# Two gate units of each long convolution in three-product form, with the split of the normalised activations woven around the convolution loop

## The chip, the core and the metric

The kernel runs on one core of a Trainium2 chip. The metric is device time in microseconds (us) from the start to the end of one execution; lower is better. The engines named below are TensorE (PE, matmuls), VectorE (DVE), ScalarE (ACT), GpSimd (POOL) and SyncE (SP, which here only issues the weight transfers). Each has its own queue, executed in the order written, and they meet through semaphores.

## What is computed

A stack of five blocks over 256 positions of width 1024, all in float32: a long-convolution mixer, a forgetting-attention mixer, a short-convolution mixer, a second long-convolution mixer, and a last block with three kinds of attention and a feed-forward part. The change touches the two long-convolution mixers alone. One of them, cut to what matters:

```python
def conformer_conv_mixer(h, w_in, conv_w, conv_b, ln_g, ln_b, w_out):   # h = rms_norm(x), 256 x 1024
    proj = h @ w_in                                   # 1024 x 6144
    val, glu_gate, z = jnp.split(proj, 3, axis=-1)    # 2048 channels each
    u = val * jax.nn.sigmoid(glu_gate)
    u = causal_depthwise_conv(u, conv_w) + conv_b     # 31 taps
    u = jax.nn.silu(layer_norm(u, ln_g, ln_b))        # over the 2048 channels
    return (u * jax.nn.silu(z)) @ w_out               # 2048 x 1024
```

## The kernel before

Activations lie transposed: channels on the partitions, the 256 positions along the free axis. So the 2048 channels of a mixer are 16 tiles of 128 x 256 (`c` = 0 to 15), and the 1024 channels of `x` are eight. Weights come in units of 1 MB (1024 x 256) through `ring`, three slots; SP issues the transfer of a unit when the unit three places before it is used up. A unit holds two halves of 128 output channels.

A product with a unit has two forms. In the **plain** form TensorE multiplies the float32 unit in `ring` by the float32 activations `sqb` (L783): 16 matmuls, each of which the profile records as two. In the **split** form both sides are first written as a high part, rounded to the type fp32r, and a low part, the difference. ACT casts a half of the unit to `whi` (L371, 128x1024), DVE or POOL subtracts to get `wlo` (L380, 128x1024), and TensorE makes three products for each of the 8 tiles of `x`: whi by xh, whi by xl, wlo by xh. That is 48 matmuls for a unit. `whi` and `wlo` have four places, so a half is cast ahead by at most four. The activations are split in four steps of two tiles: a cast to `xh` on ACT and a subtraction to `xl` on DVE (`norm_low`, 128x512, both inputs in SBUF, in blocks other than this one).

A long-convolution mixer (`plan_conf`, `conf_pe`, `conf_act`, `conf_dve`, `conf_pool`; `j` = 0 for the first, 1 for the second) has three parts.

1. **The loop** over `c`. TensorE makes value and gate of tile `c` (units `vg`, plain); ACT takes the sigmoid, DVE multiplies to `up`. The 31 taps are shared: DVE adds up 20 of them in PSUM (L1191), ACT scales the other 11 (L1043) into four buffers `tmp`, and POOL adds those (L1101, and L1104 as the last, which counts `pool_sum`). DVE joins the two sums (`join`); the last tile, 15, is joined at L1147 and L1149. ACT squares each finished tile (L1022), and TensorE adds tiles and squares over the channels two tiles at a time (`pair_sums(q)`, L1256); `pair_sums(7)` needs tile 15. Beside that, TensorE makes the eight units `z` (gate of the output): two within the loop, six behind it.
2. **Statistics**, beside units `z[4]` and `z[5]`. ACT copies the sums (L1057), TensorE turns them (`stats_turned`, L1261 and L1262), DVE reduces them and makes the variance (L1207 to L1210), ACT takes the root (L1059, behind an `ACT_TABLE_LOAD`), DVE the reciprocal, and TensorE spreads mean and factor to all partitions (`spread(0)`, `spread(1)`, L1266). The places of these matmuls among those of `z[5]` are written as `at_k={(half, k): ...}`.
3. **The y loop** over the 16 tiles, in pairs `q` on DVE: `centre` (L1225) and multiply by the factor (L1237), then ACT's silu (L1072), then POOL's product with silu(z) into the three slots `yr` (L1110), then ACT's cast to `y_hi` (`y_high`, L958), then DVE's subtraction to `y_lo` (`y_low`, L962). POOL may write a slot only when the `y_low` three tiles before is done. Into the same loops are written the splits of the first two units of `w_out` (`OUT_BESIDE`: unit 0 at c = 8, unit 1 at c = 13), two casts on ACT and two subtractions on DVE each. The splits of the other units of `w_out` come behind the loops. TensorE meanwhile makes `z[5]`, `z[6]`, `z[7]` and then the eight units of `w_out` (L865 to L867, split), 5.8 us each.

## Time and profile before

| | |
|---|---|
| median of 3 runs | 1489.11 us (1487.85 to 1490.62) |
| the profiled execution | 1488.68 us |
| its span, first to last instruction | 1486.8 us |
| TensorE | 1463.6 us busy, 98% |
| VectorE | 1063.7 us, 72% |
| ScalarE | 843.3 us, 57% |
| GpSimd | 470.1 us, 32% |
| mean granted TensorE clock | 0.997 of full speed |
| first long convolution | about 10 to 238 us of the span |
| second long convolution | about 742 to 962 us |

The busy shares are averages over all blocks. What a change is worth has to be read at its own place, from the order of time of each engine there, from the waits, and from the chain of work that ended last: that chain is followed back from the last instruction, at each step to what released it.

### The profile page before, as it was taken

Reading aid. Unit: us, or ns where it says so; the run is one execution under the profiler, and the core shown is the slowest. Engines: PE = TensorE matmul, PEld = TensorE weight load, DVE = VectorE, ACT = ScalarE, POOL = GpSimd, SP = SyncE. Lnnn points to the kernel's source line nnn. Section 1 sums busy time; section 2 is a strip of 40 time slices with the busy share of each in tenths; the row PEclk is TensorE's granted clock in tenths of the full one; section 3 lists DMA queues with packets and bytes.
Section 4 is the critical chain, followed back from the end, with each engine's and each line's share of the span. In section 5 each row is a group of like instructions: output and inputs, shape, how many; then the busy total and the mean of one; then the engine's idle time right before and its main releaser. Section 6 shows DMA issues by size and latency. Waiting matters only on the chain.

```text
span 1486.8 us, 24998 instructions
## 1 busy us (share of the span) xinstructions
PE 1463.6 (98%) x9231; PEld 1299.2 (87%) x9231; DVE 1063.7 (72%) x2225; ACT 843.3 (57%) x1612; POOL 470.1 (32%) x447
## 2 busy tenths in 40 slices
PE   8999999999999999999999999999999999999999
PEld 6888899998889988889988888999887778988887
DVE  5899767455787698887599997565257677786632
ACT  4567766445666555555456777454336756556542
POOL 2778613433333200000057883054421002000033
PEclk9999999999999999999999999998999999999999
DMA  7554355766644567876454445563852224576653
GB/s 212 150 165 149 126 188 173 232 168 151 129 142 151 158 186 208 220 196 200 143 142 142 142 142 170 185 165 114 213 158 86 86 86 141 148 205 187 173 196 112
DMA packets 308110, 239.40 MB, mean 161 GB/s; under 512 B 18018, under 2 KB 286708, under 8 KB 307989
## 3 DMA queue, kind: packets, MB, share of 16 engines
q1 hardware_dynamic: 295816, 228.70, 52.7%
q10 hardware_dynamic: 12172, 9.10, 2.7%
q8 instruction: 74, 1.21, 0.4%
q14 instruction: 48, 0.39, 0.1%
HBM read 236.02 MB, written 1.75 MB: 160 GB/s over the span
## 4 chain that ended last, share of the span: by engine, by line
PE 65%; DVE 24%; issue 5%; ACT 4%; POOL 2%; DMA 1%; DVEq 0%; POOLq 0%; SPq 0%; ACTq 0%
PE bank L805 12%; DVE bank L1191 11%; PE bank L807 6%; PE bank L865 3%; PE bank L867 3%; PE bank L866 3%; DVE wlo L380 3%; PE bank L783 3%; PE bank L1719 3%; PE bank L1721 3%; PE bank L1720 3%; PE bank L2079 2%; PE bank L1346 2%; PE bank L828 2%; PE bank L787 1%
## 5 line engine op out<-in xcount | busy, mean ns | idle before, releaser
L380 POOL TENSOR_TENSOR wlo<-ring,whi 128x1024 fp32r<-128x1024 f32 x89 | 222.4, 2506 | 861.7 <-ACT whi L371 861.7
L371 ACT CAST whi<-ring 128x1024 fp32r<-128x1024 f32 x330 | 338.4, 1046 | 193.9 <-PE bank L1721 49.5
L380 DVE TENSOR_TENSOR wlo<-ring,whi 128x1024 fp32r<-128x1024 f32 (+1 forms) x241 | 296.2, 1249 | 147.0 <-ACT whi L371 146.3
L783 PE MATMUL bank<-sqb,ring 128*128 128x256 f32 x1504 | 331.8, 380 | 1.0 <-DVE sqb L662 0.8
L783 PEld LDWEIGHTS bank<-sqb,ring 128*128 128x128 f32 x1504 | 283.7, 190 | 47.7 <-issue 6.4
L805 PE MATMUL bank<-xhl,whi 128*128 128x512 f32 x768 | 269.1, 395 | 1.3 <-DVE xhl L708 1.3
L1191 DVE SCALAR_TENSOR_TENSOR bank<-scratch,convw,bank 128x256 f32<-128x256 f32 x600 | 240.6, 484 | 0.0
L1101 POOL TENSOR_TENSOR scratch<-scratch 128x256 f32<-128x256 f32 x288 | 199.7, 732 | 98.4 <-ACT scratch L1043 74.8
L807 PE MATMUL bank<-xhl,wlo 128*128 128x256 f32 x768 | 215.2, 280 | 0.0
L805 PEld LDWEIGHTS bank<-xhl,whi 128*128 128x128 f32 x768 | 143.9, 187 | 35.0 <-issue 2.0
L1043 ACT ACTIVATE scratch<-scratch,convw 128x256 f32<-128x256 f32 x320 | 146.2, 499 | 47.8 <-POOL scratch L1101 47.0
L865 PE MATMUL bank<-y_hi,whi 128*128 128x256 f32 x512 | 146.1, 285 | 1.8 <-DVE wlo L380 1.8
L807 PEld LDWEIGHTS bank<-xhl,wlo 128*128 128x128 f32 x768 | 145.1, 189 | 0.0
L866 PE MATMUL bank<-y_lo,whi 128*128 128x256 f32 x512 | 144.8, 283 | 0.0
L867 PE MATMUL bank<-y_hi,wlo 128*128 128x256 f32 x512 | 144.8, 283 | 0.0
L1719 PE MATMUL bank<-xhl,whi 128*128 128x256 f32 x384 | 110.2, 287 | 0.8 <-DVE qk L1679 0.8
L1720 PE MATMUL bank<-xhl,whi 128*128 128x256 f32 x384 | 108.6, 283 | 0.0
L1721 PE MATMUL bank<-xhl,wlo 128*128 128x256 f32 x384 | 108.5, 283 | 0.0
L865 PEld LDWEIGHTS bank<-y_hi,whi 128*128 128x128 f32 x512 | 98.2, 192 | 2.7 <-ACT whi L371 2.1
L866 PEld LDWEIGHTS bank<-y_lo,whi 128*128 128x128 f32 x512 | 98.2, 192 | 0.1
L867 PEld LDWEIGHTS bank<-y_hi,wlo 128*128 128x128 f32 x512 | 98.2, 192 | 0.0
L1394 ACT ACTIVATE scratch<-scratch,small 128x128 f32<-128x128 f32 (+1 forms) x120 | 50.9, 425 | 46.8 <-DVE small L1384 46.8
(322 smaller groups left out, 2747.8 us busy)
## 6 DMA issues: line engine op xcount, KB each, us to landing
ring<-in_a_w_in_dram SPq DMA_DIRECT2D x64, 512.0 KB, 5.2
ring<-in_b_w_in_dram SPq DMA_DIRECT2D x32, 1024.0 KB, 6.0
ring<-in_c_w_in_dram SPq DMA_DIRECT2D x64, 512.0 KB, 5.3
ring<-in_w_in_dram SPq DMA_DIRECT2D x26, 1024.0 KB, 5.2
ring<-in_w_ffn_in_dram SPq DMA_DIRECT2D x44, 512.0 KB, 5.0
ring<-in_a_w_in_dram SPq DMA_DIRECT2D x16, 1024.0 KB, 5.1
ring<-in_a_w_out_dram SPq DMA_DIRECT2D x16, 1024.0 KB, 5.4
ring<-in_w_ffn_out_dram SPq DMA_DIRECT2D x10, 1024.0 KB, 5.0
```

Source lines behind the costliest of these rows:

```text
L371: nc.scalar.copy(piece(whi, h)[:, :, 0:n], src).then_inc(hi_done, 1)
L380: engine.tensor_tensor(piece(wlo, h)[:, :, 0:n], src, piece(whi, h)[:, :, 0:n].bitcast(F32), ALU.subtract).then_inc(done, 1)
L783: mm = nc.tensor.matmul(o, halves[h][1][:, k, :], sqb[:, k, :], start=(k == 0), stop=(k == KD - 1))
L805: nc.tensor.matmul(o[:, :], wh[:, k, :], xhl[:, k, :, :].rearrange("p s t -> p (s t)"), start=(k == 0), stop=False, skip_group_check=True)
L807: mm = nc.tensor.matmul(o[:, 0:S], wl[:, k, :], xh[:, k, :], start=False, stop=(k == KD - 1), skip_group_check=True)
L865: nc.tensor.matmul(o, wh[:, k, :], hi[:, kk, :], start=first, stop=False, skip_group_check=True)
L866: nc.tensor.matmul(o, wh[:, k, :], lo[:, kk, :], start=False, stop=False, skip_group_check=True)
L867: mm = nc.tensor.matmul(o, wl[:, k, :], hi[:, kk, :], start=False, stop=end, skip_group_check=True)
L1101: nc.gpsimd.tensor_tensor(to, a, tmp[:, (first + i) % 4, :], ALU.add)\
L1191: ins = nc.vector.scalar_tensor_tensor(to[:, a, :], src, w, to[:, a, :], ALU.mult, ALU.add)
L1719: nc.tensor.matmul(o, wh, xh[:, k, :], start=first, stop=False, skip_group_check=True)
L1720: nc.tensor.matmul(o, wh, xl[:, k, :], start=False, stop=False, skip_group_check=True)
```

## The change

- Units `z[6]` and `z[7]` of both mixers are made in split form (`Z_SPLIT`). All four low parts of the unit halves are DVE's.
- The activations are therefore split in this block too: the four casts to `xh` stand on ACT in the loop, behind the taps of tiles 8, 9, 11 and 12 (`X_HIGHS`); three of the four subtractions to `xl` stand on DVE ahead of the join of tile 15, the fourth behind it.
- ACT casts the first half of `z[6]` between the squares of tiles 14 and 15, the second half behind the load of the root's table, both halves of `z[7]` behind the root. DVE subtracts the first half of `z[6]` ahead of the statistics, and the other three in the y loop, at q = 1, 2 and 3 (`Z_LOWS`).
- ACT copies the sums ahead of the load of the root's table, not behind it, and `stats_turned`, `spread(0)` and `spread(1)` stand two plain matmuls (four recorded ones) earlier in `z[5]`.
- The calls `act_ahead` and `dve_ahead` of the loop stay only for tile 0 of the second mixer; at the others they issued nothing.
- `RESPLIT`, the list by which the splits of the activations are counted, has all six blocks now; the one wait written with a fixed number follows it.

```diff
+        Z_SPLIT = (6, 7)
...
-                n["z"].append((free, unit_in(w, [(2 * E + i * 2 * P, 2 * P)], plain=True)))
+                n["z"].append((free, unit_in(w, [(2 * E + i * 2 * P, 2 * P)], ALL if i in Z_SPLIT else False, plain=(i not in Z_SPLIT))))
...
-        RESPLIT = (1, 2, 4, 5)
+        RESPLIT = (0, 1, 2, 3, 4, 5)
...
+        X_HIGHS = (8, 9, 11, 12)
...
+                if c in X_HIGHS:
+                    g = X_HIGHS.index(c)
+                    act.wait_ge(xr_done, KD * n["ph"] + 2 * g + 2)
+                    if j == 1:
+                        group_done(act, n["vg"][0][1])
+                    nc.scalar.copy(xh[:, 2 * g:2 * g + 2, :], sqb[:, 2 * g:2 * g + 2, :]).then_inc(xh_done, 1)
...
-            for c in range(KE - 2, KE):
-                square(c)
+            square(KE - 2)
+            hi_to(act, first_half[n["z"][6][1]])
+            square(KE - 1)
             conf_z(act, n, 4)
-            nc.scalar.activation(l_warm, eps, ACT.Sqrt)
             act.wait_ge(sqm_done, (j + 1) * (KE // 2))
             nc.scalar.copy(x_sums, bank[7][:, 0:S]).then_inc(mean_done, 1)
+            nc.scalar.activation(l_warm, eps, ACT.Sqrt)
+            hi_to(act, last(n["z"][6][1]))
             act.wait_ge(var_done, j + 1)
             nc.scalar.activation(l_var, l_var, ACT.Sqrt, bias=eps).then_inc(lstd_done, 1)
+            hi_to(act, last(n["z"][7][1]))
...
+            for g in range(3):
+                norm_low(dve, n["ph"], g)
             join(len(TILE_GROUPS) - 1)
+            norm_low(dve, n["ph"], 3)
+            lo_dve_to(dve, first_half[n["z"][6][1]])
             dve.wait_ge(stat_tr, j + 1)
...
+            Z_LOWS = {1: last(n["z"][6][1]), 2: first_half[n["z"][7][1]], 3: last(n["z"][7][1])}
...
             for q in range(KE // 2 + 2):
+                if q in Z_LOWS:
+                    lo_dve_to(dve, Z_LOWS[q])
...
-            proj_T(pe, *n["z"][5], at_k={(0, 2): lambda: pair_sums(7), (0, 7): stats_turned, (1, 3): lambda: spread(0), (1, 6): lambda: spread(1)})
-            proj_T(pe, *n["z"][6])
+            proj_T(pe, *n["z"][5], at_k={(0, 2): lambda: pair_sums(7), (0, 5): stats_turned, (1, 1): lambda: spread(0), (1, 4): lambda: spread(1)})
+            proj_T(pe, *n["z"][6], True, n["ph"])
             proj_T(pe, *n["z"][7])
```

How the queues stand at the three places that matter. First DVE in the first mixer, from the last taps to the fourth pair of the y loop. Before (L1147 and L1149 are the join of tile 15, L1207 the first step of the statistics, L1225 `centre`, L1237 the multiplication, L962 `y_low`):

```order
L1191 SCALAR_TENSOR_TENSOR bank<-scratch,convw,bank 128x256 x12
L1147 TENSOR_TENSOR wide<-bank,scratch 128x256
L1149 TENSOR_TENSOR wide<-bank,wide 128x256
L1207 TENSOR_REDUCE small<-bank 128x4
...
L1225 TENSOR_TENSOR wide<-wide,bank 128x512 x3
L1237 TENSOR_TENSOR wide<-wide,bank 128x512
L1225 TENSOR_TENSOR wide<-wide,bank 128x512
L1237 TENSOR_TENSOR wide<-wide,bank 128x512
L962 TENSOR_TENSOR y_lo<-yr,y_hi 128x256
```

The same place on DVE with the change (L710 is `norm_low`, L1160 and L1162 the join, L1224 the statistics, L1242 `centre`, L1257 the multiplication, L964 `y_low`):

```order
L1204 SCALAR_TENSOR_TENSOR bank<-scratch,convw,bank 128x256 x12
L710 TENSOR_TENSOR xhl<-sqb,xhl 128x2x256 x3
L1160 TENSOR_TENSOR wide<-bank,scratch 128x256
L1162 TENSOR_TENSOR wide<-bank,wide 128x256
L710 TENSOR_TENSOR xhl<-sqb,xhl 128x2x256
L380 TENSOR_TENSOR wlo<-ring,whi 128x1024
L1224 TENSOR_REDUCE small<-bank 128x4
...
L1257 TENSOR_TENSOR wide<-wide,bank 128x512
L380 TENSOR_TENSOR wlo<-ring,whi 128x1024
L1242 TENSOR_TENSOR wide<-wide,bank 128x512
L1257 TENSOR_TENSOR wide<-wide,bank 128x512
L964 TENSOR_TENSOR y_lo<-yr,y_hi 128x256
L380 TENSOR_TENSOR wlo<-ring,whi 128x1024
```

Three subtractions have come ahead of the join, two instructions between it and the statistics, and a subtraction of a unit half ahead of the second, third and fourth pair.

Second, ACT at the statistics of the first mixer. Before (L990 is silu of z, L1022 a square, L1055 the load of the root's table and a dummy root, L1057 the copy of the sums, L1059 the root, L1072 the silu of the y loop):

```order
L1022 ACTIVATE scratch<-wide 128x256 x2
L990 ACTIVATE wide<-bank 128x512
L1055 ACT_TABLE_LOAD
L1055 ACTIVATE small<-small 128x1
L1057 COPY rr<-bank 128x256
L1059 ACTIVATE small<-small 128x2
L1072 ACT_TABLE_LOAD
```

With the change, on ACT (L1025 is the square, L993 silu of z, L1066 the copy, L1067 the table and the dummy, L1070 the root, L1084 the silu of the y loop):

```order
L1025 ACTIVATE scratch<-wide 128x256
L371 CAST whi<-ring 128x1024
L1025 ACTIVATE scratch<-wide 128x256
L993 ACTIVATE wide<-bank 128x512
L1066 COPY rr<-bank 128x256
L1067 ACT_TABLE_LOAD
L1067 ACTIVATE small<-small 128x1
L371 CAST whi<-ring 128x1024
L1070 ACTIVATE small<-small 128x2
L371 CAST whi<-ring 128x1024 x2
L1084 ACT_TABLE_LOAD
```

The copy has moved ahead of the table load, and four casts of unit halves stand around it and the root.

Third, TensorE in `z[5]`. Before (L1256 is the end of `pair_sums(7)`, L1261 and L1262 `stats_turned`, L1266 the two spreads, L783 plain matmuls, L865 the first of `w_out`):

```order
L1256 MATMUL bank<-scratch,cst 32x256 x2
L783 MATMUL bank<-sqb,ring 128x256 x5
L1261 MATMUL bank<-cst,rr 128x128
L1262 MATMUL bank<-cst,rr 128x128
L783 MATMUL bank<-sqb,ring 128x256 x4
L1266 MATMUL bank<-scratch,cst 128x256
L783 MATMUL bank<-sqb,ring 128x256 x3
L1266 MATMUL bank<-scratch,cst 128x256
L783 MATMUL bank<-sqb,ring 128x256 x33
L865 MATMUL bank<-y_hi,whi 128x256
```

And with the change, on TensorE (L785 is the plain matmul, L1281, L1282 and L1286 are the statistics, L789 to L791 the three products of the split form):

```order
L1276 MATMUL bank<-scratch,cst 32x256 x2
L785 MATMUL bank<-sqb,ring 128x256 x3
L1281 MATMUL bank<-cst,rr 128x128
L1282 MATMUL bank<-cst,rr 128x128
L785 MATMUL bank<-sqb,ring 128x256 x4
L1286 MATMUL bank<-scratch,cst 128x256
L785 MATMUL bank<-sqb,ring 128x256 x3
L1286 MATMUL bank<-scratch,cst 128x256
L785 MATMUL bank<-sqb,ring 128x256 x3
L789 MATMUL bank<-xhl,whi 128x256
L790 MATMUL bank<-xhl,whi 128x256
L791 MATMUL bank<-xhl,wlo 128x256
```

Three plain matmuls now stand between the pair sums and `stats_turned` where five stood, and 96 split matmuls stand where 32 plain ones did.

## Rows read from the trace of the kernel before

**Rows 1.** The page: the chain that ended last, share by engine.
```profile
PE 65%; DVE 24%; issue 5%; ACT 4%; POOL 2%; DMA 1%; DVEq 0%; POOLq 0%; SPq 0%; ACTq 0%
```

**Rows 2.** TensorE in order: start, us, engine, line, operation, count, idle time before and releaser.
```profile
168.63 0.41 PE L1256 MATMUL bank<-wide,cst 128*32 128x256 f32 x2 [0.61 <-ACT scratch L1022]
...
175.57 14.41 PE L783 MATMUL bank<-sqb,ring 128*128 128x256 f32 x66
...
193.04 0.28 PE L865 MATMUL bank<-y_hi,whi 128*128 128x256 f32 x1
193.16 0.28 PE L866 MATMUL bank<-y_lo,whi 128*128 128x256 f32 x1
...
202.62 0.36 PE L865 MATMUL bank<-y_hi,whi 128*128 128x256 f32 x1 [0.89 <-DVE wlo L380]
```

**Rows 3.** The chain that ended last, 182 to 203 us: start, us, what.
```profile
182.48 0.61 DVE wide L1237
183.11 0.61 ACT wide L1072
183.81 0.77 POOL yr L1110
...
185.00 0.95 ACT whi L371
...
200.18 1.05 ACT whi L371
201.25 1.24 DVE wlo L380
```

**Rows 4.** DVE in order of time, 160 to 187 us.
```profile
160.24 4.79 DVE L1191 SCALAR_TENSOR_TENSOR bank<-scratch,convw,bank 128x256 f32<-128x256 f32 x12
167.16 0.42 DVE L1147 TENSOR_TENSOR wide<-bank,scratch 128x256 f32<-128x256 f32 x1 [2.13 <-POOL scratch L1104]
...
171.88 0.17 DVE L1207 TENSOR_REDUCE small<-bank 128x4 f32<-128x8 f32 x1 [3.85 <-PE bank L1262]
...
178.97 0.49 DVE L962 TENSOR_TENSOR y_lo<-yr,y_hi 128x256 fp32r<-128x256 f32 x1 [0.72 <-ACT y_hi L958]
...
181.20 0.68 DVE L962 TENSOR_TENSOR y_lo<-yr,y_hi 128x256 fp32r<-128x256 f32 x1 [0.19 <-ACT y_hi L958]
...
185.98 2.36 DVE L380 TENSOR_TENSOR wlo<-ring,whi 128x1024 fp32r<-128x1024 f32 x2 [0.81 <-ACT whi L371]
```

**Rows 5.** ACT in order of time, at the statistics.
```profile
170.40 0.35 ACT L1057 COPY rr<-bank 128x256 f32<-128x256 f32 x1
172.68 0.30 ACT L1059 ACTIVATE small<-small 128x2 f32<-128x2 f32 x1 [1.93 <-DVE small L1210]
```

**Rows 6.** POOL in order of time: the adds of tile 15, and one product.
```profile
160.10 6.22 POOL L1101 TENSOR_TENSOR scratch<-scratch 128x256 f32<-128x256 f32 x9 [0.23 <-DVE wide L1145]
166.40 0.73 POOL L1104 TENSOR_TENSOR scratch<-scratch 128x256 f32<-128x256 f32 x1
...
195.86 1.47 POOL L1110 TENSOR_TENSOR yr<-wide 128x256 f32<-128x256 f32 x1 [2.04 <-ACT wide L1072]
```

**Rows 7.** DVE twice, POOL once: the same four subtractions in two other blocks.
```profile
531.00 2.49 DVE L708 TENSOR_TENSOR xhl<-sqb,xhl 128x512 fp32r<-128x512 f32 x4
...
989.14 6.45 DVE L708 TENSOR_TENSOR xhl<-sqb,xhl 128x512 fp32r<-128x512 f32 x4 [2.84 <-ACT xhl L704]
988.66 2.37 POOL L380 TENSOR_TENSOR wlo<-ring,whi 128x1024 fp32r<-128x1024 f32 x1 [1.65 <-ACT whi L371]
```

**Rows 8.** ACT, then DVE, in order of time, where tile 12 enters the loop.
```profile
116.44 1.28 ACT L990 ACT_TABLE_LOAD   x1
...
120.06 0.42 DVE L1131 TENSOR_TENSOR scratch<-bank,scratch 128x256 f32<-128x256 f32 x1 [0.57 <-ACT scratch L1011]
```

**Rows 9.** TensorE in the second long convolution, in order of time.
```profile
893.26 0.41 PE L1256 MATMUL bank<-wide,cst 128*32 128x256 f32 x2 [0.63 <-ACT scratch L1022]
...
900.20 14.41 PE L783 MATMUL bank<-sqb,ring 128*128 128x256 f32 x66
```

7 lines of the change are left out of this document (4 added, 3 removed).

## The prediction

> **What bounds the kernel now.** The page's busy shares would name TensorE, and the shares of the chain name it too, but they give VectorE a quarter of the chain [rows 1]. So the place of the change is read by itself, in four steps.
>
> First, TensorE in order of time. From the end of the loop to the output product it waits twice: 0.61 us for the square of tile 15 and 0.89 us for a low part of w_out's third unit [rows 2]. In between it is busy with the plain matmuls of z[5] to z[7]. That is the picture of an engine with next to no slack, and it invites the sum "cheaper z units, earlier end".
>
> Second, what released the wait of 0.89 us. The chain through this stretch does not run over TensorE at all: it goes from a multiplication on DVE to the silu on ACT, the product on POOL, the cast on ACT, a cast and a subtraction of a unit half, and so on, until ACT casts the third unit of w_out at 200.18 us and DVE subtracts it at 201.25 us [rows 3]. That cast stands behind the whole y loop in ACT's queue. So the third unit of w_out starts at the end of the y loop plus 2.4 us, whatever TensorE has done by then. The y loop sets the end; TensorE merely arrives 0.89 us early.
>
> Third, what sets the start of the y loop: the join of tile 15 at 167.16 us, for which DVE waited 2.13 us [rows 4] because POOL's adds of that tile ended at 167.13 us [rows 6]; then square, pair sums and statistics.
>
> Fourth, the second mixer. Its waits and its z stretch are the same (0.63 us, and 66 records in 14.41 us) [rows 9], so each term below counts twice.
>
> **TensorE's own gain.** z[6] and z[7] hold 64 of the 66 recorded plain matmuls: 64 x 14.41/66 = 14.0 us [rows 2]. The 96 split ones come at the spacing of the output product, 193.16 - 193.04 = 0.12 us, so 11.5 us. TensorE has 2.5 us less to do in each mixer, 5.0 us in all. This is worth something only if the y loop ends earlier too.
>
> **The statistics.** Copy, turn and spreads stand four recorded matmuls earlier: 4 x 0.218 = 0.87 us. The copy was done at 170.40 + 0.35 = 170.75 us and the root waited 1.93 us for its input [rows 5], so here it was TensorE's queue that held the statistics back, and moving the places gives -0.87 us at the start of the y loop. Putting the copy ahead of the table load only makes that possible; alone it gives nothing. The cast of the second half of z[6] stands ahead of the root. By the row it ends some 1.05 us behind the dummy root, before or about when the variance is ready, so I take 0 for it.
>
> **The join of tile 15.** Three subtractions of 128x512 now stand ahead of the join. At 2.49/4 = 0.62 us each [rows 7] they need 1.9 us and would fit in the idle 2.13 us [rows 4]. But the same four instructions took 6.45 us, 1.61 us each, while POOL ran a subtraction of its own of 2.37 us [rows 7], and a product on POOL, 0.73 us when alone, took 1.47 us when DVE was in a subtraction [rows 6]. The taps of the loop, which read PSUM and run beside POOL all the time, do not show this. So where both engines work from two inputs in SBUF, one waits for the other. Ahead of the join this hits the worst spot: POOL is in its last two adds and the sum, the work that DVE's join waits for. Taken in turn, three subtractions at 0.6 us and three of POOL's at 6.22/9 = 0.69 us, less the small overlaps at the ends, last about 3.5 us from 165.0 us: the join comes at 168.4 us instead of 167.16 us, **+1.2 us**. Bounds: 0, if they interleave freely, and 3 x 1.61 - 2.13 = +2.7 us, if each is drawn out as in the slow row. I take 1.2, since POOL's pieces here are short, unlike those of the slow row.
>
> The Trainium skill states the mechanism outright (SBUF — State Buffer, Who interferes with whom): a VectorE instruction with two SBUF inputs contends with a GpSimd instruction that reads SBUF, the port pair is locked for a whole instruction, and the other engine blocks. By it the term is +1.2 us as reckoned; without it the term would be 0, and the sum 2.4 us lower over the two mixers. It speaks against this placement, and the three rows agree with it.
>
> The fourth subtraction and the first unit half stand behind the join: 0.6 + 1.2 us, inside the 3.85 us for which DVE waited for the turned sums [rows 4]: 0. If that cover went, they would cost up to 1.8 us.
>
> **The casts to xh in the loop.** Four of about 0.6 us on ACT. Three fall where ACT waits for POOL or TensorE anyway. The one behind tile 9 stands ahead of the first taps of tile 10 and of the table load at 116.44 us, behind which DVE waits 0.57 us for a sigmoid [rows 8]. DVE has no slack there, and what it loses it keeps up to the join. ACT has about 0.3 us of short waits ahead of that load, so I take **+0.2 us**, bounds 0 and 0.6.
>
> **The y loop.** Three subtractions of unit halves stand on DVE at q = 1, 2, 3, 1.14 us each (2.36 us for two with the tail of the last) [rows 4]: +3.4 us ahead of the multiplication at 182.48 us, which is on the chain [rows 3]. DVE was idle 0.72 and 0.19 us there, waiting for ACT [rows 4]; its results would now be ready when it comes, so 0.9 us is absorbed. The low part at 181.20 us took 0.68 us, beside a product on POOL, against 0.49 at 178.97 us [rows 4]; it no longer meets that product: another 0.2 us. Net **+2.3 us**. From that multiplication on the chain goes through ACT, POOL, ACT again and DVE as before [rows 3], and nothing in it gets shorter. Bounds: +1.7, if the 0.81 us that DVE waits at 185.98 us [rows 4] is absorbed as well, and +3.4, if nothing is.
>
> ACT's casts of z[7] follow the root and are over, with a table load of 1.28 us as in [rows 8], by about 176.6 us, before the first silu at 177.1: 0. TensorE needs the low parts of z[6] and z[7] later than DVE makes them: 0. The new ring order only frees slots earlier: 0.
>
> **The sum.** For one mixer: -0.87 + 1.2 + 0.2 + 2.3 = +2.8 us at the end of the y loop, so at the third unit of w_out. Behind that TensorE runs without a wait to the end of the stage and passes the delay on. TensorE's own 2.5 us become waiting: at the pair sums (0.61 us grows to 2.0), at the second unit and at the third. Twice +2.8 = +5.6 us. On the profiled execution's 1488.68 us that is **1494.3 us**. The median of the runs shown is 0.43 us above that execution, which the range takes in.
>
> **The rivals.**
>
> *The contention is mild (22%).* The subtractions ahead of the join fit in the idle 2.13 us. For it: the plain length, 1.9 us. Against: the 6.45 and the 1.47 us. One mixer: -0.87 + 0.2 + 2.3 = +1.6, in all +3.2: 1491.9 us. With the y loop at its lower bound and no cost for the casts it is (1.7 - 0.87) x 2 = +1.7: 1490.4 us.
>
> *The contention is heavy (16%).* The join is 2.7 us late: +4.3 for one mixer, +8.6 in all: 1497.3 us.
>
> *TensorE is the bound after all (14%): faster.* Mechanism: the three subtractions in the y loop vanish into waits of DVE, and the y loop ends 2.5 us earlier, so that TensorE's shorter z units count in full: -5.0 us, 1483.7 us. For it: TensorE waits only 1.5 us in this stretch. Against: it needs the loop to lose 2.5 us, and the only thing that makes it shorter is the 0.87 us. It decides at 3.4 us of idle time of DVE ahead of 182.48 us; the rows show 0.9.
>
> *The change doesn't do what it says.* If the turned sums still waited for something else, such as the copy behind the late pair sums, the -0.87 would be 0 and the sum 1.7 us higher, 1496.0 us. It lies within the range.
>
> **How the numbers follow.** My forecast has 48%, mild contention 22%, heavy 16%, TensorE as the bound 14%. The range leaves out the last and takes in the others with their bounds: from 1490.4 less the scatter of the runs, 1489.0, to 1498.0. A measurement can tell 0.2%, 3.0 us, from no change, so faster is below 1486.1 us and slower above 1492.1. Slower: 47 of the 48, all of the heavy case, and 9 of the 22: 72%. Faster: 13%. Within: 15%.
>
> **What would show it.** In the changed kernel's trace, in each mixer: the wait of DVE at the join gone or shorter and the join itself some 1.4 us later; the subtractions to xl longer than 0.68 us and one of POOL's last adds longer than 0.73 us; TensorE waiting 2 us at the last pair sums; the turned sums at about 172, not 171.5 us; the split z units at 11.5 us; the wait of 0.89 us at the third unit of w_out grown to about 4 us, part of it moved to the second unit, still released by DVE's low part; and that unit starting near 205.4 us. I am wrong if that unit starts before 202.6 us, or if the wait there is gone.

## The result: 0.5% slower, and the profile after

| | before | changed kernel |
|---|---|---|
| median | 1488.57 us (6 runs, 1487.74 to 1490.62) | 1495.57 us (6 runs, 1492.78 to 1498.46) |
| profiled execution | 1488.68 us | 1495.07 us |
| its span | 1486.8 us | 1493.3 us |
| TensorE busy | 1463.6 us | 1461.8 us |
| VectorE busy | 1063.7 us | 1077.0 us |

The ratio is 1.0049, 95% interval 1.0035 to 1.0062: slower by 7.0 us (5.2 to 9.2), where 5.6 us was predicted. TensorE has less to do and the kernel takes longer.

**The join.** First DVE in the changed kernel, first mixer, in order of time (start, us, engine, line, operation, count, idle time before and its releaser), then POOL. L710 are the subtractions to xl, L1160 is the join, L1224 the first step of the statistics, L1257 at 184.77 the multiplication that stood at 182.48 us on the chain [rows 3].

```profile
160.16 4.79 DVE L1204 SCALAR_TENSOR_TENSOR bank<-scratch,convw,bank 128x256 f32<-128x256 f32 x12
164.86 3.52 DVE L710 TENSOR_TENSOR xhl<-sqb,xhl 128x512 fp32r<-128x512 f32 x3
168.30 0.41 DVE L1160 TENSOR_TENSOR wide<-bank,scratch 128x256 f32<-128x256 f32 x1
...
172.16 0.17 DVE L1224 TENSOR_REDUCE small<-bank 128x4 f32<-128x8 f32 x1 [1.25 <-PE bank L1282]
...
177.25 1.22 DVE L380 TENSOR_TENSOR wlo<-ring,whi 128x1024 fp32r<-128x1024 f32 x1
...
179.97 1.21 DVE L380 TENSOR_TENSOR wlo<-ring,whi 128x1024 fp32r<-128x1024 f32 x1
...
183.03 1.21 DVE L380 TENSOR_TENSOR wlo<-ring,whi 128x1024 fp32r<-128x1024 f32 x1
184.17 0.67 DVE L1242 TENSOR_TENSOR wide<-wide,bank 128x512 f32<-128x512 f32 x1
184.77 0.67 DVE L1257 TENSOR_TENSOR wide<-wide,bank 128x512 f32<-128x512 f32 x1
```

```profile
160.00 6.70 POOL L1113 TENSOR_TENSOR scratch<-scratch 128x256 f32<-128x256 f32 x9 [0.21 <-DVE wide L1158]
166.78 1.05 POOL L1116 TENSOR_TENSOR scratch<-scratch 128x256 f32<-128x256 f32 x1
```

DVE no longer waits at the join, as it did for 2.13 us [rows 4]: the three subtractions, 1.9 us of work, took 3.5 us beside POOL, whose last sum took 1.05 us, not 0.73, and whose nine adds took 6.70 us, not 6.22 [rows 6]. Counted from the start of the taps the join comes at 168.30 - 160.16 = 8.14 us, before at 167.16 - 160.24 = 6.92 us [rows 4]: +1.22 us.

**TensorE** in the first mixer. L1276 is `pair_sums(7)`, L789 the first split matmul of z[6], L867 the first product of a matmul group of w_out.

```profile
169.77 0.41 PE L1276 MATMUL bank<-wide,cst 128*32 128x256 f32 x2 [1.84 <-ACT scratch L1025]
...
176.95 0.47 PE L789 MATMUL bank<-xhl,whi 128*128 128x256 f32 x1
...
189.64 0.36 PE L867 MATMUL bank<-y_hi,whi 128*128 128x256 f32 x1 [0.83 <-ACT whi L371]
...
192.97 0.39 PE L867 MATMUL bank<-y_hi,whi 128*128 128x256 f32 x1 [0.59 <-DVE y_lo L964]
...
198.06 0.36 PE L867 MATMUL bank<-y_hi,whi 128*128 128x256 f32 x1 [1.60 <-DVE wlo L380]
...
204.96 0.36 PE L867 MATMUL bank<-y_hi,whi 128*128 128x256 f32 x1 [0.92 <-DVE wlo L380]
```

Two waits of together 1.50 us [rows 2] have become five of together 5.78 us, 4.28 us more: 2.42 us of that is the delay itself, and the rest, 1.9 us, is what is seen of the 2.5 us that TensorE has less to do. The row at 204.96 us is the third unit of w_out, at 202.62 us before [rows 2].

**The second mixer.** The same rows of TensorE, and the busy time of the engines in stretches of 5 us (PEclk is the granted clock).

```profile
899.16 0.41 PE L1276 MATMUL bank<-wide,cst 128*32 128x256 f32 x2 [1.82 <-ACT scratch L1025]
...
899.73 2.49 PE L785 MATMUL bank<-sqb,ring 128*128 128x256 f32 x6
```

```profile
core 0: us, PE busy (x) PEld busy (x) DVE busy (x) ACT busy (x) POOL busy (x), PEclk, DMA share, GB/s
895.00:900.00 5.00, 3.18 (x20) 2.17 (x19) 4.97 (x7) 1.93 (x4) 2.15 (x2) 1.00 0.57 182
900.00:905.00 5.00, 5.00 (x18) 4.03 (x18) 1.97 (x10) 4.17 (x7) 0.00 (x0) 0.66 0.09 28
905.00:910.00 5.00, 5.00 (x32) 4.61 (x30) 4.17 (x6) 3.03 (x4) 0.89 (x1) 1.00 0.10 21
```

Behind TensorE's wait of 1.82 us the granted clock falls: 0.66 in 900 to 905 us, a mix of the two levels, 2.4 and 1.2 GHz. The six recorded matmuls behind the pair sums took 2.49 us, where the same six in the first mixer, at full clock, took 1.56 us (from 170.34 us), and the turned sums, for which the statistics wait, stand right behind them.

**The account.** Since each part begins where the last ends, three distances say where the time went: start of the taps to join, join to first step of the statistics, and from there to the third unit of w_out, behind which TensorE passes any delay on.

| us, first mixer | before | after | difference | predicted |
|---|---|---|---|---|
| taps to join | 6.92 | 8.14 | +1.22 | +1.2 |
| join to statistics (168.30 to 172.16) | 4.72 | 3.86 | -0.86 | -0.87 |
| statistics to third unit | 30.74 | 32.80 | +2.06 | +2.3 |
| casts ahead of the taps | | | 0 | +0.2 |
| sum | | | +2.4 | +2.8 |

The second mixer adds +2.4 us and 1.65 us for the lower clock (join to third unit 38.32 us there, 36.66 in the first). Both: 6.5 us. The two profiled executions differ by 6.4 us, but the rest of their span is not equal either: the short-convolution block, which the change leaves alone, took 3.0 us less in the one execution of before, and other stretches 3.0 us more, 2.3 of it behind the second mixer, where both have some lower clock between 1000 and 1050 us. The kernel before, run again, had the same 221.0 us as the changed kernel from the table load at 523 us to the one at 744 us, where the first trace had 218.0. Over all fourteen traces of this case that block took 218.0 us in four and 221.0 us in ten, with nothing between. So that belongs to the execution, not to the kernel, and I compare distances within a mixer from here on.

### The profile page after: what moved, and what is told of

Its sections match the earlier page's. It is cut to its first block, busy times and chain, and to the rows that moved or that the text cites. A ratio compares the mean times of both kernels' runs of the same rounds, so it can differ in the third digit from the quotient of the medians.

```text
span 1493.3 us, 25180 instructions
## 1 busy us (share of the span) xinstructions
PE 1461.8 (98%) x9295; PEld 1297.6 (87%) x9295; DVE 1077.0 (72%) x2241; ACT 853.4 (57%) x1628; POOL 475.6 (32%) x447
## 3 DMA queue, kind: packets, MB, share of 16 engines
q8 instruction: 74, 1.21, 0.3%
## 4 chain that ended last, share of the span: by engine, by line
PE 68%; DVE 23%; ACT 4%; issue 2%; POOL 1%; DMA 1%; ACTq 1%; DVEq 0%; POOLq 0%; SPq 0%
PE bank L807 12%; DVE bank L1204 10%; PE bank L809 6%; PE bank L785 4%; PE bank L867 3%; PE bank L869 3%; PE bank L868 3%; DVE wlo L380 3%; PE bank L1739 3%; PE bank L1741 3%; PE bank L1740 3%; PE bank L1366 2%; PE bank L2099 2%; PE bank L830 2%; PE bank L789 1%
## 5 line engine op out<-in xcount | busy, mean ns | idle before, releaser
L371 ACT CAST whi<-ring 128x1024 fp32r<-128x1024 f32 x338 | 346.8, 1046 | 193.4 <-PE bank L1741 49.5
L380 DVE TENSOR_TENSOR wlo<-ring,whi 128x1024 fp32r<-128x1024 f32 (+1 forms) x249 | 305.7, 1247 | 146.7 <-ACT whi L371 145.9
L785 PE MATMUL bank<-sqb,ring 128*128 128x256 f32 x1376 | 305.7, 382 | 1.0 <-DVE sqb L664 0.8
L785 PEld LDWEIGHTS bank<-sqb,ring 128*128 128x128 f32 x1376 | 260.4, 191 | 44.6 <-issue 6.4
L807 PEld LDWEIGHTS bank<-xhl,whi 128*128 128x128 f32 x768 | 144.2, 188 | 37.4 <-issue 2.1
L867 PE MATMUL bank<-y_hi,whi 128*128 128x256 f32 x512 | 146.1, 285 | 7.9 <-DVE wlo L380 5.0
L867 PEld LDWEIGHTS bank<-y_hi,whi 128*128 128x128 f32 x512 | 98.2, 192 | 9.4 <-ACT whi L371 7.7
L1739 PEld LDWEIGHTS bank<-xhl,whi 128*128 128x128 f32 x384 | 73.5, 191 | 3.8 <-ACT whi L371 2.5
```

The lines of the kernel that those rows point to most:

```text
L371: nc.scalar.copy(piece(whi, h)[:, :, 0:n], src).then_inc(hi_done, 1)
L380: engine.tensor_tensor(piece(wlo, h)[:, :, 0:n], src, piece(whi, h)[:, :, 0:n].bitcast(F32), ALU.subtract).then_inc(done, 1)
L785: mm = nc.tensor.matmul(o, halves[h][1][:, k, :], sqb[:, k, :], start=(k == 0), stop=(k == KD - 1))
L807: nc.tensor.matmul(o[:, :], wh[:, k, :], xhl[:, k, :, :].rearrange("p s t -> p (s t)"), start=(k == 0), stop=False, skip_group_check=True)
L867: nc.tensor.matmul(o, wh[:, k, :], hi[:, kk, :], start=first, stop=False, skip_group_check=True)
L1739: nc.tensor.matmul(o, wh, xh[:, k, :], start=first, stop=False, skip_group_check=True)
```

## The experiments

The chief measure is **join to third unit**, in us, first and second mixer, beside the ratio to the kernel before, run beside it, with its 95% interval, and the wait of TensorE at `pair_sums(7)` (one number where both mixers have the same). Theory: the loss is DVE and POOL blocking each other ahead of the join (+1.2 us a mixer) plus three low parts in the y loop (+2.1), less the earlier statistics (-0.86); TensorE's shorter units are worth nothing there. Chief rivals: the contention is no part of it, or TensorE's time does count.

| run | join to third unit | wait at pair sums | median us | ratio |
|---|---|---|---|---|
| before again | 35.45 / 35.45 | 0.6 | 1488.16 (one) | |
| change again | 38.30 / 36.67 | 2.4 | 1496.78 | 1.0050 (1.0032 to 1.0068) |
| one SBUF input | 36.67 / 36.66 | 0.65 | 1491.22 | 1.0015 (1.0004 to 1.0027) |
| statistics alone | 34.60 / 34.60 | 0.6 | 1487.10 | 0.9989 (0.9978 to 0.9999) |
| z[6] alone | 34.89 / 34.91 | 1.8, 2.4 | 1490.90 | 1.0019 (1.0005 to 1.0032) |
| two lows on POOL | 39.27 / 39.46 | 1.8, 2.4 | 1500.08 | 1.0075 (1.0056 to 1.0095) |
| split of x alone | 35.46 / 37.15 | 2.4 | 1494.32 | 1.0033 (1.0019 to 1.0047) |
| nothing added on DVE's path | 35.93 / 35.94 | 0.6 | 1489.63 | 1.0000 (0.9988 to 1.0012) |
| five ahead of the join | 35.46 / 35.46 | 2.0 | 1493.79 | 1.0034 (1.0020 to 1.0048) |
| ten ahead of the join | 38.32 / 37.50 | 5.6 | 1500.33 (one) | |
| low parts later | 34.63 / 34.64 | 0.6 | 1485.87 | 0.9989 (0.9977 to 1.0001) |
| statistics earlier still | 34.24 / 34.25 | 0.6 | 1485.29 | 0.9986 (0.9974 to 0.9998) |

### The two kernels again

> The kernel before, unchanged, for a second trace of it. Only 2 x 2.3 us of the 6.5 us by which the changed kernel's span is longer lie at the two third units of w_out (204.96 against 202.62 us in the first mixer). The rest lies elsewhere: +3.0 us in the short-convolution block, whose code is the same, 0.21 us for each of its 14 tiles; +1.7 us in a stretch of the second mixer with a granted clock of 0.91; and -1.3 us where only the trace of before had such a stretch. Theory A, these belong to the single execution: this second trace of the same kernel shows 0.21 us for a tile, or the place of the slow clock stretches, differently from the first. Theory B, they belong to the kernel: this trace shows 11.09 us for a tile of the short block (as before) and the changed kernel's next one 11.30.

> The changed kernel, unchanged, for a second trace of it and three more rounds of times. Theory A (see the run of the kernel before): third unit of w_out at 205.0 us again, since that is set by the order of the queues, but the pace of the short block and the slow clock stretches come out otherwise than in its first trace. Theory B: the short block at 11.30 us for a tile again. Time against before: 1.003 to 1.006 by either; the two queue terms alone give 4.7 us, 1.0031.

The kernel before gave the same distances, the changed one a second pattern. Its DVE, then its POOL, then TensorE, first mixer:

```profile
165.46 1.89 DVE L710 TENSOR_TENSOR xhl<-sqb,xhl 128x512 fp32r<-128x512 f32 x3
169.45 0.42 DVE L1160 TENSOR_TENSOR wide<-bank,scratch 128x256 f32<-128x256 f32 x1 [2.10 <-POOL scratch L1116]
```

```profile
160.61 8.01 POOL L1113 TENSOR_TENSOR scratch<-scratch 128x256 f32<-128x256 f32 x9 [0.22 <-DVE wide L1158]
168.69 0.72 POOL L1116 TENSOR_TENSOR scratch<-scratch 128x256 f32<-128x256 f32 x1
```

```profile
170.93 0.60 PE L1276 MATMUL bank<-wide,cst 128*32 128x256 f32 x2 [2.40 <-ACT scratch L1025]
```

Here DVE's three subtractions ran at full pace, 1.89 us, and POOL was the one held up: nine adds in 8.01 us, not 6.22 [rows 6]. DVE's wait at the join is back, 2.10 us, and looks as if nothing had happened; but the join comes 3.91 us behind the end of the taps, 3.35 us in the first trace of the change, 2.13 us before. So the same code costs 1.2 or 1.8 us here, and who is blocked changes from execution to execution. The third unit, expected at 205.0 us again, came at 207.75 us: the later join is one part of that, and a stretch of lower clock behind the wait of 2.40 us another, 1.6 us (38.30 us against the second mixer's 36.67).

### Is it the two SBUF inputs?

The subtractions to xl take their second input from PSUM, so the low parts of x are not computed: same count, shape and place.

```diff
+            def one_input(g):
+                dve.wait_ge(xh_done, 4 * RESPLIT.index(n["ph"]) + g + 1)
+                nc.vector.tensor_tensor(xl[:, 2 * g:2 * g + 2, :], sqb[:, 2 * g:2 * g + 2, :],
+                                        shift.unsqueeze(1).to_broadcast((P, 2, S)), ALU.subtract).then_inc(xn_done, 1)
+
             for g in range(3):
-                norm_low(dve, n["ph"], g)
+                one_input(g)
             join(len(TILE_GROUPS) - 1)
-            norm_low(dve, n["ph"], 3)
+            one_input(3)
```

> The changed kernel with the four subtractions to xl reading one input from SBUF and the other from PSUM (the shift in bank 3, in place of xh), same shape, same places. What it leaves out: xl is not the low part, so z units 6 and 7 are computed from a wrong low part; all other work stands. My theory: what makes the join of tile 15 late is not the 1.9 us that three such subtractions take, but that DVE and POOL both work from two SBUF inputs; with one input each takes 0.6 us, the three end at 166.8 us, before POOL's sum, and the join is back at 167.2 us, 1.1 us earlier than the 168.3 us of the changed kernel; the third unit of w_out starts at 203.8 us; 2.3 us less in all, ratio to before about 1.0015 to 1.004. Rival: DVE is late simply because it has 1.9 us more work and POOL is late because ACT supplies its taps later (casts in the loop): then nothing changes, join at 168.3 us, third unit at 205.0 us.

DVE and POOL of that run, first mixer:

```profile
165.37 1.87 DVE L1219 TENSOR_TENSOR xhl<-sqb,bank 128x512 fp32r<-128x512 f32 x3
167.60 0.42 DVE L1160 TENSOR_TENSOR wide<-bank,scratch 128x256 f32<-128x256 f32 x1 [0.36 <-POOL scratch L1116]
```

```profile
160.51 6.25 POOL L1113 TENSOR_TENSOR scratch<-scratch 128x256 f32<-128x256 f32 x9 [0.21 <-DVE wide L1158]
```

Both engines run at full pace and the subtractions fit in the idle time, the join 2.14 us behind the end of the taps. TensorE's wait is back to 0.65 us, and of 1.0050 there remains 1.0015. The rest, 2.2 us, is the y loop less the statistics, 2 x (36.67 - 35.45) = 2.4 us. So the blocking is shown, and with all that hangs on it it costs about 5 us of the 7 (the means of the two kernels, run side by side, differ by 5.2 us, 95% within 2.8 to 7.5), where 2.4 us was reckoned for both mixers. The traces account for 3.5 to 4.7 us of it: 1.2 or 1.8 us a mixer, and 1.1 us on average for the clock.

The Trainium skill (SBUF — State Buffer, Who interferes with whom) states that a VectorE instruction with at most one SBUF input, outside the modes that use two ports for one tensor, doesn't contend with GpSimd, and that one with two SBUF inputs does, with a GpSimd instruction that reads SBUF. These runs agree: 1.87 us beside 6.25 us in the one case, 3.52 beside 6.70 or 1.89 beside 8.01 in the other. It also says that the issue order decides who blocks; no run here tests that for the two patterns.

The converse, the change's split of x alone, with z[6] and z[7] plain and the statistics where they were:

```diff
-                n["z"].append((free, unit_in(w, [(2 * E + i * 2 * P, 2 * P)], ALL if i in Z_SPLIT else False, plain=(i not in Z_SPLIT))))
+                n["z"].append((free, unit_in(w, [(2 * E + i * 2 * P, 2 * P)], plain=True)))
...
-            hi_to(act, first_half[n["z"][6][1]])
...
-            hi_to(act, last(n["z"][6][1]))
...
-            hi_to(act, last(n["z"][7][1]))
...
-            lo_dve_to(dve, first_half[n["z"][6][1]])
...
-                if q in Z_LOWS:
-                    lo_dve_to(dve, Z_LOWS[q])
```

> The kernel before with one part alone: the casts to xh in the loop and the subtractions to xl around the join of tile 15. z stays plain (xh and xl are made and not used), the statistics stand as before. My theory: DVE and POOL block each other ahead of the join; join 1.2 to 1.8 us late in each mixer, TensorE's wait at the last pair sums 1.8 to 2.4 us in place of 0.61, and from the join to the third unit of w_out 35.46 us as before; +2.5 to +3.6 us in all, ratio 1.0017 to 1.0024, and up to 1.7 us more for each mixer in which the granted clock falls behind that wait, as it did in two of the four stretches of the changed kernel seen so far. Rival, that the casts in ACT's queue or the mere 1.9 us of DVE cost: join at most 0.3 us late, ratio 1.000.

From the end of the taps to the join it took 3.90 us in both mixers, POOL's nine adds 8.00 us, and join to third unit was exactly that of before in the first, but 37.15 us in the second, where the clock fell. The split of x by itself is 0.33% slower, above the 0.17 to 0.24% expected without the clock: the two joins make 3.5 us of the 4.9.

### The statistics alone

```diff
-            nc.scalar.activation(l_warm, eps, ACT.Sqrt)
             act.wait_ge(sqm_done, (j + 1) * (KE // 2))
             nc.scalar.copy(x_sums, bank[7][:, 0:S]).then_inc(mean_done, 1)
+            nc.scalar.activation(l_warm, eps, ACT.Sqrt)
...
-            ... (0, 7): stats_turned, (1, 3): lambda: spread(0), (1, 6): lambda: spread(1)})
+            ... (0, 5): stats_turned, (1, 1): lambda: spread(0), (1, 4): lambda: spread(1)})
```

> The kernel before with one part of the change alone: the copy of the sums ahead of the load of the root's table, and turn and spreads two plain matmuls earlier in z[5]. z stays plain, nothing else moves. My theory: the y loop starts 0.87 us earlier and ends 0.87 us earlier (third unit of w_out at 201.8 us, TensorE's wait there from 0.89 to 0.02 us): -1.7 us in all, ratio 0.9988. Rival, in which TensorE is the bound there: it has as many matmuls as before and waited only 0.89 us, so at most the same is gained; the two agree on the end but differ on the wait ahead of the pair sums, which stays 0.61 us by mine. Second rival, in which this part does nothing because the copy comes too late: turned sums at 171.9 us and third unit at 202.6 us as before, 0.

Join to third unit fell from 35.45 to 34.60 us, 0.85 us, where the prediction had 0.87. TensorE's waits there:

```profile
169.56 0.41 PE L1256 MATMUL bank<-wide,cst 128*32 128x256 f32 x2 [0.62 <-ACT scratch L1022]
...
202.69 0.36 PE L865 MATMUL bank<-y_hi,whi 128*128 128x256 f32 x1 [0.27 <-DVE wlo L380]
```

This piece of the change is a gain, 0.11%. The wait at the third unit has shrunk from 0.89 to 0.27 us, so TensorE has almost caught up with the y loop.

### One split unit in place of two

```diff
-        Z_SPLIT = (6, 7)
+        Z_SPLIT = (6,)
...
-            hi_to(act, last(n["z"][7][1]))
...
-            Z_LOWS = {1: last(n["z"][6][1]), 2: first_half[n["z"][7][1]], 3: last(n["z"][7][1])}
+            Z_LOWS = {1: last(n["z"][6][1])}
```

> The changed kernel with z[7] plain again, so one subtraction of a unit half is left in the y loop (q = 1) and two are gone (q = 2, 3). From the join to the third unit of w_out it takes 35.46 us before and 36.67 with the change. My theory, the y loop on DVE sets the end: the one subtraction left falls into DVE's idle 0.9 us, so the distance is about 34.9 us, 1.8 less than with the change and 0.3 more than the 34.60 us of the kernel with the earlier statistics alone; the join stays late by 1.2 to 1.8 us; 3.6 us less than the change in all, ratio to before about 1.001 to 1.0025. Rival, TensorE's split form is the cost (its low parts come late): removing half of the split units halves the extra over the earlier statistics, 36.67 - 34.60 = 2.07, to about 35.6 us. Rival, TensorE is the bound: z[7] plain costs 1.25 us more and the distance grows to 37.9 us.

Join to third unit is 34.90 us, as expected, and neither 35.6 nor 37.9 us. From statistics to third unit it is 31.03 us, 0.29 more than before: the first low part costs next to nothing, which fits DVE's waits of 0.72 and 0.19 us in the y loop [rows 4]. The other two of the change cost 0.89 us each.

### Low parts on POOL, two misses

The second half of z[6] and the first of z[7] go to POOL, which is idle between the taps and the y loop.

```diff
-                n["z"].append((free, unit_in(w, [(2 * E + i * 2 * P, 2 * P)], ALL if i in Z_SPLIT else False, plain=(i not in Z_SPLIT))))
+                n["z"].append((free, unit_in(w, [(2 * E + i * 2 * P, 2 * P)], {6: "first", 7: "second"}.get(i, False), plain=(i not in Z_SPLIT))))
...
+            lo_pool_to(pool, last(n["z"][7][1]))
...
-            Z_LOWS = {1: last(n["z"][6][1]), 2: first_half[n["z"][7][1]], 3: last(n["z"][7][1])}
+            Z_LOWS = {3: last(n["z"][7][1])}
```

> The changed kernel with the low parts of the second half of z[6] and the first half of z[7] made by POOL between its last sum and its first product of the y loop, where it is idle for 10 us, in place of DVE at q = 1 and 2. TensorE does the same as with the change. My theory: only DVE's time in the y loop counts; with one subtraction left there (q = 3) the distance from the join to the third unit of w_out is 34.9 to 35.2 us in place of 36.67, though both z units are split; ratio to before about 1.001 to 1.003. Rival, that the split form costs by itself on TensorE: 36.67 us as with the change. Where I may be off: POOL takes 2.4 us for each half, is done with the second at about 178.1 us, and its first product may start up to 0.5 us late.

Slower than the change itself. DVE, POOL and TensorE in the first mixer:

```profile
173.72 0.17 DVE L1225 TENSOR_REDUCE small<-bank 128x4 f32<-128x8 f32 x1 [2.49 <-PE bank L1283]
173.93 2.14 DVE L1226 TENSOR_SCALAR small<-small 128x2 f32<-128x2 f32 x1
176.10 0.16 DVE L1227 TENSOR_TENSOR small<-small 128x2 f32<-128x2 f32 x1
...
185.43 1.76 DVE L380 TENSOR_TENSOR wlo<-ring,whi 128x1024 fp32r<-128x1024 f32 x1
```

```profile
173.69 2.35 POOL L380 TENSOR_TENSOR wlo<-ring,whi 128x1024 fp32r<-128x1024 f32 x1 [5.53 <-ACT whi L371]
```

```profile
176.90 0.70 PE L1287 MATMUL bank<-scratch,cst 128*128 128x256 f32 x2 [1.04 <-DVE scratch L1232]
```

The step that multiplies two numbers per partition, 0.17 us in the change, took 2.14 us: it ended with POOL's subtraction, at 176.07 us against 176.04. I had looked at DVE's large instructions for contention and at its statistics only for length. And the low part at q = 3 took 1.76 us beside POOL's products, where it took 1.21 in the change. In this mixer the clock fell as well, behind the wait of 1.81 us at the pair sums. In the second mixer the 128x2 step was spared; there two diagonals, `TENSOR_SCALAR` on 128x128, took 4.38 us instead of 0.48 beside POOL's two subtractions (4.65 us), TensorE waited 2.58 us for them, and the clock fell behind that wait (0.50 in 912.5 to 915 us).

Next a kernel that adds nothing to DVE's path: z[6] alone split, both low parts on POOL, the four subtractions to xl behind the join, the statistics eight recorded matmuls earlier than before.

```diff
-        Z_SPLIT = (6, 7)
+        Z_SPLIT = (6,)
...
-            hi_to(act, last(n["z"][6][1]))
...
-            hi_to(act, last(n["z"][7][1]))
+            hi_to(act, last(n["z"][6][1]))
...
+            pool.wait_ge(xn_done, 4 * RESPLIT.index(n["ph"]) + 4)
+            lo_pool_to(pool, last(n["z"][6][1]))
...
-            for g in range(3):
+            join(len(TILE_GROUPS) - 1)
+            for g in range(4):
                 norm_low(dve, n["ph"], g)
-            join(len(TILE_GROUPS) - 1)
-            norm_low(dve, n["ph"], 3)
-            lo_dve_to(dve, first_half[n["z"][6][1]])
...
-            Z_LOWS = {1: last(n["z"][6][1]), 2: first_half[n["z"][7][1]], 3: last(n["z"][7][1])}
...
-            ... (0, 5): stats_turned, (1, 1): lambda: spread(0), (1, 4): lambda: spread(1)})
+            ... (0, 3): stats_turned, (0, 7): lambda: spread(0), (1, 2): lambda: spread(1)})
```

> A version that uses the findings: z[6] split and z[7] plain; all four subtractions to xl behind the join, where POOL is idle; both low parts of z[6] on POOL behind them; no subtraction of a unit half added to DVE; the second cast of z[6] behind the root; turn and spreads four plain matmuls earlier than before (two earlier than in the change). My theory: join at its old distance from the last taps (2.2 us), from the join to the third unit of w_out 35.46 - 8 x 0.2155 = 33.7 us, TensorE arriving there just in time thanks to 1.25 us less for z[6]: -1.7 us in each mixer, -3.4 us in all, ratio 0.9977. Rival, TensorE bounds once the y loop is shorter than before by 0.9 us: distance 34.6 us or more, ratio 0.9988. Where it can go wrong: the subtractions behind the join (2.4 us) hold up DVE's first step of the statistics, which would add up to 0.5 us.

The same trap. DVE, then POOL, first mixer:

```profile
172.47 2.34 DVE L1224 TENSOR_SCALAR small<-small 128x2 f32<-128x2 f32 x1
```

```profile
172.44 2.34 POOL L380 TENSOR_TENSOR wlo<-ring,whi 128x1024 fp32r<-128x1024 f32 x1 [3.40 <-DVE xhl L710]
```

TensorE waited 1.81 us for the first diagonal. Of the 33.7 us expected from join to third unit it missed by 2.2 us in each mixer; the ratio is 1.0000.

The Trainium skill (SBUF — State Buffer, Who interferes with whom) names `tensor_scalar` among the instructions that can take the port pair shared with GpSimd, one of the two then blocking for a whole instruction. The two rows agree: 2.14 and 2.34 us, the rest of POOL's instruction, for 0.17 us of work.

### The clock behind TensorE's wait

Four of ten mixers in which TensorE waited 1.8 us or longer at the pair sums had a stretch of lower clock behind it. Is it the wait, or something that the change does? The kernel before, with five or ten DVE instructions ahead of the join that read one operand from SBUF, write where nobody reads, and leave POOL its pace (its nine adds took 6.23 us in the second mixer, 6.22 before):

```diff
+            for g in range(5):
+                chain(dve, nc.vector.tensor_tensor(xl[:, 2 * (g % 4):2 * (g % 4) + 2, :], sqb[:, 2 * (g % 4):2 * (g % 4) + 2, :],
+                                        shift.unsqueeze(1).to_broadcast((P, 2, S)), ALU.subtract))
             join(len(TILE_GROUPS) - 1)
```

> The question is the clock. In the runs so far a stretch of lower granted clock followed TensorE's wait at the last pair sums in 4 of 10 mixers where that wait was 1.8 us or longer, and in 0 of 10 where it was 0.6 us. This kernel is the one before with nothing but five extra DVE instructions ahead of the join of tile 15: sqb minus a PSUM tile, written to a buffer that nobody reads in this block, so without the blocking between DVE and POOL, and without split units, casts or moved statistics. They need about 5 x 0.7 = 3.5 us and DVE was idle for 2.13 us there, so the join should come 1.4 to 1.6 us later and TensorE's wait at the last pair sums should be 2.0 to 2.2 us, not 0.6. Theory: the wait alone brings the clock down. Then each mixer has four chances in ten of a stretch near 0.66 behind the pair sums, which puts 1.65 us more between the join and the third unit of w_out (35.45 us becomes 37.1), and the kernel costs 2 x 1.5 = 3.0 us plus 1.3 us on average: ratio 1.0025 to 1.0035. Rival: the fall needs something of the change itself (split units, casts on ACT, the blocked DVE or POOL). Then the clock stays near 1, the distance is 35.45 us in both mixers, and the ratio is 1.002.

> The same kernel with ten extra DVE instructions in the place of five: 10 x 0.7 = 7 us for 2.13 us of idle time, so the join comes about 5 us later and TensorE waits 5.4 to 5.8 us at the last pair sums. Theory, the wait brings the clock down: with a wait nearly three times as long the stretch of lower clock should be there in both mixers, 1.65 us or more each between join and third unit. Rival, the length of the wait doesn't matter or something of the change itself is needed: no stretch in either mixer, the distance 35.45 us, and the time 10 us above the kernel before. One miss and one hit would leave it open.

With five the waits were 2.01 and 2.00 us and both stretches stayed at 1.00: no fall in the traced execution. The timed runs cost 5.0 us (3.0 to 7.1), where the late joins alone make 2 x 1.4. In the traced execution, 4.9 us longer than the second trace of the kernel before (spans 1491.2 and 1486.3 us), the rest stands ahead of anything that was changed: its first mixer ends its taps at 166.90 us, against 164.67, and traces of three other kernels start as late. What the timed runs add to the joins stays open. The timed executions have no trace, but each has a mean granted clock: two of the seven have 0.995 (1495.0 and 1495.6 us) and five 0.998 (1491.1 to 1493.9 us). Of the kernel before no execution out of 81 in the three groups of runs lies below 0.996, nor does one of the 57 of the five kernels whose pair sums come on time; of the 45 of the kernels with a late join twelve do. With ten, TensorE of the first mixer and the stretches around it:

```profile
173.29 0.64 PE L1259 MATMUL bank<-wide,cst 128*32 128x256 f32 x2 [5.62 <-ACT scratch L1022]
```

```profile
165.00:170.00 5.00, 2.68 (x13) 2.01 (x11) 4.76 (x8) 0.28 (x1) 1.70 (x3) 1.00 0.49 153
170.00:175.00 5.00, 1.71 (x10) 0.84 (x11) 2.56 (x5) 2.24 (x4) 0.00 (x0) 0.74 0.16 57
175.00:180.00 5.00, 5.00 (x16) 4.02 (x15) 0.50 (x3) 0.41 (x2) 0.00 (x0) 0.58 0.00 0
180.00:185.00 5.00, 5.00 (x25) 4.41 (x24) 4.17 (x11) 1.97 (x3) 0.00 (x0) 1.00 0.04 9
```

The clock fell in both mixers, and join to third unit grew by 2.9 and 2.0 us. So a wait of 5.6 us is enough, with nothing of the change in the kernel, and the mean clocks point to the same for 2 us, in part of the executions. Over all traces:

| TensorE's wait at the pair sums | mixers | with a lower clock behind it | cost on the path |
|---|---|---|---|
| 0.58 to 0.65 us | 14 | 0 | |
| 1.8 to 2.4 us | 12 | 4 | 1.6 to 1.7 us in three; the fourth, with two low parts on POOL, meets other waits |
| 5.6 us | 2 | 2 | 2.0 and 2.9 us |

### Two versions that keep the gain

The kernel that added nothing to DVE's path, with POOL's low parts held back until DVE is through the statistics:

```diff
-            pool.wait_ge(xn_done, 4 * RESPLIT.index(n["ph"]) + 4)
+            pool.wait_ge(stat_diag, 4 * j + 4)
```

> The version with only z[6] in split form, all xl subtractions behind the join, both low parts on POOL and the statistics eight recorded matmuls earlier, but with POOL's first low part held back until all four diagonals of the statistics are written. My reading of the version without that wait: 2.2 us were lost because DVE's tensor_scalar on 128x2 was blocked behind POOL's subtraction. With the wait that instruction takes 0.17 us again, TensorE's wait of 1.8 us for the first diagonal is gone, and the distance from the join to the third unit of w_out falls from 35.93 to between 33.8 and 34.3 us (POOL's second low part now ends about 0.6 us behind the moment at which its first product could start). Against the kernel before that is 2 x 1.15 to 2 x 1.65 us less: ratio 0.9978 to 0.9985, which beats the version that only moves the statistics (0.9989). Rival: POOL's low parts now meet the y loop, whose first product and first low part of y they hold up in full (2.3 us); then the distance is 36 us again and the ratio 1.0.

DVE's 128x2 step took 0.17 us again and TensorE's wait for the diagonal was gone. The distance is 34.63 us, 1.3 below the kernel without the wait and 0.3 above the range I gave. So of the 2.2 us only 1.3 came back: POOL's two subtractions now end at 178.99 us and hold up its first product of the y loop. The first cast to y_hi waits 1.14 us for that product, 0.36 us in the kernel without the wait.

And no split unit at all, only the copy ahead of the table load, as in "The statistics alone", and the statistics eight recorded matmuls earlier:

```diff
-            ... (0, 7): stats_turned, (1, 3): lambda: spread(0), (1, 6): lambda: spread(1)})
+            ... (0, 3): stats_turned, (0, 7): lambda: spread(0), (1, 2): lambda: spread(1)})
```

> No split units at all: the kernel before with the copy ahead of the table load and stats_turned and the two spreads eight recorded matmuls earlier instead of four. The version with four gave 34.60 us from join to third unit, and TensorE still waited 0.27 us at the third unit. Theory: at that point TensorE becomes the bound, because without the split z units its work between pair sums and third unit has no slack but these 0.27 us. Then four matmuls more give only 0.27 us a mixer: distance 34.33 us, the wait at the third unit gone, ratio 0.9985 at best. Only where TensorE is short of slack do the split z units have a worth of their own, and this is the place to see it against the version with z[6] split, run beside it. Rival: the y loop still sets the end, and the distance falls by another 0.87 us to 33.7 us (ratio 0.9977). Second rival: TensorE meets the turned sums or the spreads too early and waits there; then a wait appears at the transposes or the first spread and the distance is above 34.6 us.

TensorE's only wait between loop and third unit, and the third unit:

```profile
168.54 0.41 PE L1256 MATMUL bank<-wide,cst 128*32 128x256 f32 x2 [0.60 <-ACT scratch L1022]
...
201.31 0.28 PE L865 MATMUL bank<-y_hi,whi 128*128 128x256 f32 x1
```

The wait at the third unit is gone and the distance is 34.24 us (201.31 - 167.07), against 34.33 expected from the 0.27 us that were left. Here, and only here, TensorE is the bound, and a split z unit could have a worth of its own; but only 0.5 us of it: DVE starts the low part of the third unit at 199.49 us, 32.42 us behind the join (33.26 us in the version with z[6] split, whose distance is 34.63), and where TensorE waits for that low part it starts 1.37 us behind it [rows 2, rows 3], which would be 200.86 us here. At 0.9986 (0.9974 to 0.9998) this is the fastest version, and by its median it beats both kernels; the two others below 1 cannot be told from it.

## Why the prediction was right, point by point

- **What bounds the kernel**: right. The y loop set the end, and what TensorE has less to do came back as waits, 5.8 us of them where 1.5 stood.
- **The statistics**, -0.87: measured -0.86 in the change and 0.85 us alone.
- **The join**, +1.2: +1.22 in the first trace, but +1.8 in the second pattern, which "taken in turn" did not foresee: there POOL alone pays. That the first trace hit 1.2 so closely is partly luck. With all that hangs on it the join made some 5 us of the 7.
- **The casts in the loop**, +0.2: nothing. The table load behind the cast at tile 9 came at 116.36 us, 116.44 before, and DVE waits 0.58 us for the sigmoid of tile 12, 0.57 before [rows 8].
- **The y loop**, +2.3: +2.06. The steps "0.9 us is absorbed" and "another 0.2 us" were a little short: 3.4 - 2.06 = 1.3 us were.
- **The sum**, +2.8 a mixer: +2.4 in the pattern of the first trace, +3.0 in the other, so 4.8 to 6.0 us in all. The missing part is a term that the prediction did not have: the clock behind a TensorE wait of 1.8 us or longer, 1.65 us in 4 of 12 mixers, 1.1 us on average for two. The range took in the measured time because it left room for heavier contention, not for this term.
- **The signs named**: the join later (1.14 us by the clock of the trace, 1.4 said), TensorE's wait of 1.84 us (2 said), the turned sums at 171.74 us (172 said), the split z units in 11.9 us up to the end of the last (11.5 said), the waits behind of 3.94 us (4 said) but in four pieces, the first for ACT's cast, and the third unit at 204.96 (205.4 said).

**Open.** What decides within an execution whether DVE or POOL is the blocked one: both patterns occurred in the same code, and in the traces of two kernels (z[6] alone, two lows on POOL) one in each mixer (3.3 and 3.9 us from the end of the taps to the join). Whether a wait of 2 us brings the clock down by itself: the one trace made for it shows no fall, the mean clocks of two of its seven executions point to one. And what the five subtractions cost beyond the later joins, some 2 us.

## What to carry to other kernels

Before work is put into an engine's idle time, ask what that idle time waits for, and whether the new work slows that very thing: here DVE's 2.13 us were a wait for POOL, and DVE's own subtractions delayed POOL. Small instructions of a critical chain are as exposed as large ones. And a cheaper unit on an engine that isn't the bound there is worth nothing, while a longer wait of TensorE can cost more than its own length.

## What the runs showed of the hardware

- The same three subtractions beside the same adds: DVE 3.52 us and POOL 6.70, or DVE 1.89 us and POOL 8.01, changing between executions, and between the mixers of one. With one input from PSUM: 1.87 and 6.25 us.
- A DVE `TENSOR_SCALAR` on 128x2, 0.17 us alone, took 2.14 and 2.34 us beside one POOL subtraction of 128x1024, and two on 128x128 took 4.38 us, not 0.48, beside two such subtractions (4.65 us).
- The granted clock behind waits of TensorE: never below 1.00 in the 14 cases of 0.6 us, lower in 4 of the 12 cases of 1.8 to 2.4 us (0.66 in a stretch of 5 us behind 1.82 us), and 0.74 and 0.58 in the two such stretches that hold the end of a wait of 5.62 us and what follows it. The Trainium skill (TensorE: Matmul & The Clock Gate, Part 1) states that the gate follows how busy TensorE has just been, and these rows agree.
- The short-convolution block, with the same code, took 218.0 us in four traced executions (the first of the kernel before among them) and 221.0 us in ten: one execution of each of two kernels is no comparison at the size of this change.
